# Bias of the differential heads in pass A: added by VectorE as one fp32 table instead of by TensorE as three bf16 products

## The reference

```python
s = jnp.einsum('bqhmd,bkhmd->bhmqk', q.astype(f32), kd) * SCALE
bias = table[t5_bucket(kpos[None, :] - qp[:, None])]
s = s + jnp.transpose(bias, (2, 0, 1))[None, :, None]
mask = (kpos[None, :] // CHUNK) <= (qp[:, None] // CHUNK)
s = jnp.where(mask, s, NEG_INF)
p = jax.nn.softmax(s, axis=-1)
a = p[:, :, 0] - lam * p[:, :, 1]
```

## Time and profile before

| | us |
|---|---|
| median of 3 runs (2722.75 to 2724.26) | 2723.32 |
| the profiled execution, its own time | 2726.6 |
| its span, first to last instruction | 2724.9 |
| TensorE busy | 2629.2 (96%) |
| VectorE busy | 1320.5 (48%) |
| ScalarE busy | 943.9 (35%) |
| GpSimd busy | 390.3 (14%) |
| mean granted clock of TensorE, share of full | 0.992 |

### The profile page before, as it was taken

How to read it: one execution, slowest core, us unless ns; L and a number is a source line. 1 busy time by engine, 2 the same in 40 slices (tenths; PEclk the granted TensorE clock), 3 DMA queues, 4 the chain that set the end, 5 groups by cost and what they waited for, 6 DMA issues and landing times.

```text
span 2724.9 us, 37244 instructions
## 1 busy us (share of the span) xinstructions
PE 2629.2 (96%) x14873; PEld 2110.5 (77%) x14873; DVE 1320.5 (48%) x1947; ACT 943.9 (35%) x1837; POOL 390.3 (14%) x398
## 2 busy tenths in 40 slices
PE   5999999999999999999989999999999999999998
PEld 4788888889999999999975565566566556888887
DVE  3431123414443323344246677668667766655553
ACT  3122331112222222200114654664664567422221
POOL 0100001121100000011243203212311421200000
PEclk9999999999999999999989999999999999999999
DMA  3353334448776766674934055053241513544432
GB/s 107 110 170 108 109 114 138 134 135 221 213 193 180 211 179 183 180 205 141 245 109 92 17 113 126 5 121 77 58 101 34 117 50 98 172 138 136 131 126 96
DMA packets 405772, 353.67 MB, mean 130 GB/s; under 512 B 45440, under 2 KB 368968, under 8 KB 399416
## 3 DMA queue, kind: packets, MB, share of 16 engines
q1 hardware_dynamic: 396464, 332.66, 45.0%
q0 software_dynamic: 9136, 18.63, 2.0%
HBM read 250.23 MB, written 100.71 MB: 129 GB/s over the span
## 4 chain that ended last, share of the span: by engine, by line
PE 87%; ACT 4%; DVE 4%; issue 2%; DMA 2%; POOL 1%; SPq 0%; ACTq 0%; DVEq 0%; POOLq 0%
PE p_acc L837 14%; PE p_acc L839 14%; PE p_acc L838 14%; PE a_op L2056 5%; PE a_sb L2025 4%; PE a_sb L2032 4%; PE a_op L2053 4%; PE a_sa L2001 3%; PE a_sa L2006 2%; PE p_turn L868 2%; PE e_U L1393 2%; PE a_sa L2004 2%; PE e_U L1394 2%; PE e_U L1395 2%; ACT a_e L1874 1%
## 5 line engine op out<-in xcount | busy, mean ns | idle before, releaser
L837 PE MATMUL p_acc<-p_h_hi,p_w_hi 128*128 128x384 f32 (+1 forms) x1960 | 718.2, 366 | 9.1 <-DVE p_h_lo L655 5.8
L839 PE MATMUL p_acc<-p_h_hi,p_w_lo 128*128 128x384 f32 (+1 forms) x1960 | 702.7, 359 | 0.0
L838 PE MATMUL p_acc<-p_h_lo,p_w_hi 128*128 128x384 f32 (+1 forms) x1960 | 701.9, 358 | 0.0
L1896 DVE TENSOR_REDUCE a_nmax<-a_sa 128x1 f32<-128x1024 f32 (+7 forms) x384 | 347.7, 911 | 282.6 <-PE a_sa L2004 166.2
L1874 ACT ACTIVATE a_e<-a_sb 128x512 f32<-128x512 f32 (+3 forms) x640 | 315.9, 534 | 316.0 <-PE a_sb L2032 313.5
L837 PEld LDWEIGHTS p_acc<-p_h_hi,p_w_hi 128*128 128x128 f32 x1960 | 369.6, 189 | 44.7 <-issue 9.5
L839 PEld LDWEIGHTS p_acc<-p_h_hi,p_w_lo 128*128 128x128 f32 x1960 | 369.1, 188 | 31.8
L838 PEld LDWEIGHTS p_acc<-p_h_lo,p_w_hi 128*128 128x128 f32 x1960 | 369.8, 189 | 29.7
L2025 PE MATMUL a_sb<-a_q,a_k 128*128 128x512 f32 (+2 forms) x640 | 277.7, 436 | 8.7 <-ACT a_e L1874 8.5
L2032 PE MATMUL a_sb<-a_q,a_k 68*128 68x512 f32 (+2 forms) x640 | 248.6, 390 | 0.0
L641 DVE TENSOR_TENSOR p_w_lo<-p_raw,p_w_hi 128x1024 fp32r<-128x1024 f32 x98 | 137.8, 1407 | 225.2 <-ACT p_w_hi L577 225.1
(11 more groups left out here) (233 smaller groups left out, 3777.8 us busy)
## 6 DMA issues: line engine op xcount, KB each, us to landing
p_raw<-in_w_in SPq DMA_DIRECT2D x98, 512.0 KB, 5.3
s_k_raw<-in_cache_fox_k SPq DMA_DIRECT2D x32, 512.0 KB, 7.0
s_v_raw<-in_cache_fox_v SPq DMA_DIRECT2D x32, 512.0 KB, 6.4
s_k_raw<-in_cache_diff_k SPq DMA_DIRECT2D x32, 512.0 KB, 6.9
s_v_raw<-in_cache_diff_v SPq DMA_DIRECT2D x32, 512.0 KB, 6.5
a_q<-scratch_q_hi SPq DMA_DIRECT2D x32, 512.0 KB, 12.8
a_k<-scratch_k_hi SPq DMA_DIRECT2D x32, 512.0 KB, 15.1
e_pair<-scratch_gT SPq DMA_DIRECT2D x80, 192.0 KB, 2.7
```

Source lines behind the costliest of these rows:

```text
L837: nc.tensor.matmul(acc[a % 2][:, 0:n], hi, h_hi[p][:, k, at:at + n], start=(k == 0), stop=False)
L838: nc.tensor.matmul(acc[a % 2][:, 0:n], hi, h_lo[p][:, k, at:at + n], start=False, stop=False)
L839: last = nc.tensor.matmul(acc[a % 2][:, 0:n], lo, h_hi[p][:, k, at:at + n], start=False, stop=(k == DK - 1))
L1896: nc.vector.tensor_reduce(nmax[:, b % 2, c, col:col + 1], scores_of(ev[1]), axes, ALU.max, negate=True).then_inc(a_maxed, 1)
```

## The change

The band of pass A leaves TensorE. In its place VectorE adds the query-major band as one fp32 table to the scores in PSUM, ahead of the maximum. The maximum waits for the addition (`a_biased`). Pass B keeps its three products. The tables shrink accordingly: bf16 parts are made and stored of the key-major band alone, the query-major band is stored as it is (`bandQ`), and a pair loads three parts and one fp32 table.

```diff
@@ project: the tables
-            part = [t_.sb(f"part{i}", [P, 2, DIFF_HEADS, BAND], BF16) for i in range(3)]
-            rest = wide[:, :, :, 0:BAND]
+            part = [t_.sb(f"part{i}", [P, DIFF_HEADS, BAND], BF16) for i in range(3)]
+            rest = wide[:, 0, :, 0:BAND]
...
-                for y in range(2):
-                    sp.dma_start(d["band"][y, :, i].rearrange("h p n -> p h n"), part[i][:, y]).then_inc(band_stored, 16)
+                    sp.dma_start(d["bandQ"].rearrange("h p n -> p h n"), band[:, 0]).then_inc(band_stored, 16)
+                sp.dma_start(d["band"][:, i].rearrange("h p n -> p h n"), part[i][:]).then_inc(band_stored, 16)
...
-                    nc.vector.tensor_copy(part[0][:], band[:]).then_inc(band_step, 1)
+                    nc.vector.tensor_copy(part[0][:], band[:, 1]).then_inc(band_step, 1)
...
-                    nc.vector.tensor_tensor(rest, band[:], part[0][:], ALU.subtract).then_inc(band_step, 1)
+                    nc.vector.tensor_tensor(rest, band[:, 1], part[0][:], ALU.subtract).then_inc(band_step, 1)
@@ prompt_attention: buffers and loads
-        band = s.sb("band", [P, 2, 3, BAND], BF16)
+        band, band_q = s.sb("band", [P, 3, BAND], BF16), s.sb("band_q", [P, BAND])
+        s.sb("space_q", [P, P])
...
+    def banded(a):
+        b, m, t, c = a
+        tile = 4 * (b % BLOCKS) + t
+        first = max((tile - 1) * P, c * CHUNK_KEYS)
+        end = c * CHUNK_KEYS + a_width(a)
+        return (end - first, first - (tile - 1) * P) if is_diff(b) and first < end else None
...
-                for layout in range(2):
-                    for n in range(3):
-                        sp.dma_start(band[:, layout, n, :], d["band"][layout, f // 2, n]).then_inc(side_in[z], 16)
+                for n in range(3):
+                    sp.dma_start(band[:, n, :], d["band"][f // 2, n]).then_inc(side_in[z], 16)
+                sp.dma_start(band_q[:], d["bandQ"][f // 2]).then_inc(side_in[z], 16)
@@ vector: ahead of the maximum
+                if banded(A_UNITS[ev[1]]):
+                    n, at = banded(A_UNITS[ev[1]])
+                    if (m, c) == (0, 0):
+                        dve.wait_ge(side_in[1], side_total(b // BLOCKS))
+                    b0, n_b = banks(a_width(A_UNITS[ev[1]]))[-1]
+                    end = n_b + (512 if b0 else 0)
+                    square = sa[ev[1] % 2][:, end - n:end]
+                    nc.vector.tensor_tensor(square, square, band_q[:, at:at + n], ALU.add).then_inc(a_biased, 1)
+                    dve.wait_ge(a_biased, n_biased[ev[1] + 1])
@@ tensor: scores_a
-                    if is_diff(b) and tile - 1 <= kt <= tile and 0 <= at < n_b:
...
-                        adds += [(slice(at, at + n_m), band[:, 0, n, c0:c0 + n_m]) for n in range(3)]
...
                     nc.tensor.matmul(out, q1[z][m][:, qs], k1[z][m][:, k0:k0 + wide], start=True, stop=False)
-                    for cols, msk in adds:
-                        nc.tensor.matmul(out[:, cols], ident16[:], msk, start=False, stop=False)
                     last = nc.tensor.matmul(out, *high, start=False, stop=True)
```

More of the change, by code:

```diff
@@ L472, in sync @@
                     sp.wait_ge(nckS_stored, 16)
-                    sp.wait_ge(band_stored, 16 * 7)
+                    sp.wait_ge(band_stored, 16 * 5)
                 for b in range(SEQS):
@@ L594, in scalar @@
                     act.wait_ge(nckS_stored, 16)
-                    act.wait_ge(band_stored, 16 * 7)
+                    act.wait_ge(band_stored, 16 * 5)
                     act.wait_ge(turned, turn_at["F", 0, 4] + 1)
@@ L1500, in prompt_attention @@
     b_scored, e_made, w_made, multiplied = (s.sem(n) for n in ("b_scored", "e_made", "w_made", "multiplied"))
+    a_biased = s.sem("a_biased")
     e_masked, e_added, ones_made = s.sem("e_masked"), s.sem("e_added"), s.sem("ones_made")
@@ L1533, in prompt_attention @@
     two = lambda b: b % BLOCKS >= 2
+    def banded(a):
[4 more added lines that the diff above has]
+        return (end - first, first - (tile - 1) * P) if is_diff(b) and first < end else None
+    n_biased = list(itertools.accumulate([0] + [banded(a) is not None for a in A_UNITS]))
     dve_at, act_at = {}, {}
@@ L1543, in side_total @@
     def side_total(f):
-        return 16 * (6 if f % 2 else 2) * (f // 2 + 1)
+        return 16 * (4 if f % 2 else 2) * (f // 2 + 1)
     LEAD = 9
@@ L1990, in scores_a @@
                     at = kt * P - k0
-                    if is_diff(b) and tile - 1 <= kt <= tile and 0 <= at < n_b:
[L1992 to L1995, removed]
-                        adds += [(slice(at, at + n_m), band[:, 0, n, c0:c0 + n_m]) for n in range(3)]
-                    elif not is_diff(b) and kt == tile and 0 <= at < n_b:
+                    if not is_diff(b) and kt == tile and 0 <= at < n_b:
                         adds.append((slice(at, at + P), causal[:, 0]))
@@ L2029, in scores_b @@
                     for n in range(3):
-                        nc.tensor.matmul(sb_[m][:, lo:hi], ident16[:], band[:, 1, n, lo - t0 * P:hi - t0 * P],
+                        nc.tensor.matmul(sb_[m][:, lo:hi], ident16[:], band[:, n, lo - t0 * P:hi - t0 * P],
                                          start=False, stop=False)
@@ L2138 @@
                nckS=(DEC_BATCH * FOX_HEADS, PAST + DEC_SEQ), wide=(2, DIFF_HEADS, P, REL),
-               bandS=(DIFF_HEADS, DEC_SEQ, P + DEC_SEQ))
+               bandQ=(DIFF_HEADS, P, BAND), bandS=(DIFF_HEADS, DEC_SEQ, P + DEC_SEQ))
 INPUTS = ["x_prompt", "x_sample", "cache_fox_k", "cache_fox_v", "cache_fox_logf", "cache_diff_k", "cache_diff_v",
@@ L2222 @@
         d[name] = nc.dram_tensor(f"scratch_{name}", shape, F32, kind="Internal").ap()
-    d["band"] = nc.dram_tensor("scratch_band", (2, DIFF_HEADS, 3, P, BAND), BF16, kind="Internal").ap()
+    d["band"] = nc.dram_tensor("scratch_band", (DIFF_HEADS, 3, P, BAND), BF16, kind="Internal").ap()
     hybrid_step(nc, d)
```

## The result

The changed kernel took 2708.4 us in the median of four runs (2704.0 to 2712.2), the kernel before 2723.0 beside it. The ratio is 0.9945, with a 95% interval of 0.9929 to 0.9962: faster by 0.55%, 14.6 us. The direction and the range were right, the size was too large: 21 us were forecast.

A forecast was written before the change was run, and what follows sets the result against it. TensorE bounds, with gaps from a two-buffer ring of scores, maximum and exponential. Per pair 1.9 + 1.7 + 1.7 = 5.3 us, 21 us for four: 2702 us median; own range 2691 to 2715, 8-in-10 range 2687 to 2724.

The forecast's parts named there:

- What the products are worth, by starts: Pass A: a removed group saves 0.34 us at 256 columns, 0.24 at 128; 11.0 us a pair, 44 us gross.
- Additions and VectorE's queue: Pass A: additions take 0.43 or 0.30 us, the maximum follows after 0.03; VectorE busy 24.1 of the first 28 us.
- VectorE's queue is the bound: Rival: the maximum decides at every banded unit, each group costs +0.12 us (0.09 at 128 columns); 2739 us, chance 0.08.
- The sorting of the groups: A pair's 34 banded units in three classes: 1.9 us from units 0 to 13, 0 from (b), 3.4 from (c).
- class (b): Units 14, 19, 21, 27, 29, 31, 33, 39, followed at once by a unit waiting for ScalarE: saving 0.
- class (c): Units 15-18, 23, 25, 35, 37, 41, 43, 45, 47, in dense stream or ahead of release-setting pass-B scores: 1.7 + 1.7 us a pair.
- all of it is saved: Rival: the chain hides everywhere and waits shrink too; -35 to -44 us, 2679 to 2688 us, chance 0.08.
- the gain drowns in waits: Rival: the two-buffer ring bounds close units, class (c) waits too; within 5 us, 2718 to 2728 us, chance 0.15.
- The range's lower end: The forecast's own 2691 us, from 8 us a pair if waits absorb only half of class (b).
- The clock: Rival: TensorE idles more, clock at 0.50 for 27 us in each of four pairs, costing 54 us; 2756 us, chance 0.04.
- A clock under 1.00 after 1445 us: Listed sign that the prediction is wrong: TensorE's granted clock below its full level after 1445 us.
- Tables and DMA at nothing: Outside pass A: table building, the bandQ store and side loads (4 instead of 6, same bytes) change no time.

The follow-up runs named there:

- the experiment with the dense units alone: Kernel before with VectorE's addition only at units 15-18, 23, 25, 35, 37, 41, 43, 45 (and 47, not last pair), products elsewhere: 2712.6 us, ratio 0.9947.
- the mixed kernel: Kernel before with VectorE's addition, but products kept at units 2, 6, 9, 14, 19, 21, 27, 29, 31, 33, 39 and pass A's last: 2703.1 us, ratio 0.9917.

## Why the prediction was right, and where it was wrong

**What the products are worth, by starts: right.** 0.34 and 0.24 a group show as steps of that size from unit to unit. The busy column's 64 us would have been too much by nearly half.

**Additions and VectorE's queue: right.** 428 and 294 ns, a gap of 0.03, 23.4 us of 28 busy. The rival *VectorE's queue is the bound* (2739 us) is out.

**The sorting of the groups: right to 0.2 us a pair.** Undisturbed, unit 10 starts 0.84 us earlier against unit 0 (0.95 forecast), unit 13 1.86 (1.9), unit 26 3.7, unit 33 3.8 (class (b) in between gives nothing), unit 47 5.1 (5.3). Units 0 to 14 are 2.1 of it, not 1.9, and class (c) 3.0, not 3.4, as the experiment with the dense units alone shows. Four undisturbed pairs would be 19 to 20 us. The rivals *all of it is saved* and *the gain drowns in waits* are out by this. That is 2 us of the 21 mis-sized. (The range's lower end was given a wrong reason: half of class (b) would add 1.3 us a pair, 6.6 in all; the 8 us a pair need the whole of it.)

**The clock: the step that failed.** It was "Against it: in pass A of the first differential pair the clock stays at 1.00 even in a thin stretch like 1520 to 1524", with a chance of 0.04 and a price of 54 us as one case for itself. I took a fall of the clock as a case for itself, 27 us at 0.50 in every pair like the stretch from 1416; it falls for 3.4 us at a time, once for 6.8, inside the likeliest case, at a price of 0.6 to 1.6 us each (3.1 for the long one), three, six and three times in the three profiles. That took 4, 10 and 4 us of the 19, and the median came out 6 us above the forecast. A clock under 1.00 after 1445 us was on the list of what would show the prediction wrong, and it came. I had also read the wrong quantity: a stretch of before in which products stay away for 4 us says nothing of waits that this change makes longer, 1.2 to 1.6 us, and more frequent, 36 to 44.

The Trainium skill, "TensorE: Matmul & The Clock Gate" (A second HAM failure mode), says of a bf16 kernel that cycles through PSUM banks that frequent short idles between groups of matmuls make the clock swing between its levels. I wrote that the trace spoke against it. The trace of before did, with its 36 waits and no fall; the trace after agrees with it, with 44 waits and a fall in two of four passes. Its direction was right here, and the 54 us that I had hung on it were five to fourteen times too much.

**Tables and DMA at nothing: not contradicted.** The gaps between the passes are unchanged to 0.1 us, and nothing between 174 us and the attention has grown. The words "the same bytes" were wrong: a pair's side loads were 6 of 64 KB and are now 3 of 64 and one of 128, 320 KB instead of 384; no wait shows it. The 7 us that stand ahead of unit 0 in the profiled execution look like chance and not like the change: the start of the attention varied from 17 to 27 us at 0.50, in one kernel (the mixed one) from profile to profile, and the kernel before varied from 2719.6 to 2731.0 us in 15 runs on one chip. Without them the profiled execution would have lain some 6.6 us above the 2705.6 forecast for it, as the median does above its own. A gain outside pass A was also a sign of being wrong; this one counts neither for nor against.

## What to carry to other kernels

Price a removed operation unit by unit, by whether TensorE's stream goes on behind it or a wait takes its place; work of TensorE that ends in a wait for another engine is free, and may hold the clock up (no fall in pass A in two profiles). Remove it where the stream is dense and leave it where the wait is: the mixed kernel keeps a third of the products and is the fastest of those that compute the full result. And in a queue that runs in order, work that is ready belongs ahead of an instruction that will wait: the running sum that looked like a delay was cover, and moving it cost 16 us without the additions and 32 with them.

## What of the hardware was not expected

TensorE's granted clock can drop to 0.50, the 1.2 GHz level of its two, for about 3.4 us and come back, in the midst of pass A: in the second one TensorE is busy 108.9 of 118 us, and its longest wait is 1.6 us. What it did before one fall is above: waits of 0.82 and 0.31 us within 2 us, in a pair whose twin had the same and did not fall. An addition of two fp32 operands, one in PSUM and one in SBUF, back into PSUM in place, takes 428 ns at 256 columns and 294 at 128.
